# RWKV scan: backward operand rows with exchanged halves, and the Gram products of both directions side by side

## The reference, cut to what matters

```python
def rwkv7_scan(r, w, k, v, kk, a, s0):
    def step(s, inp):
        rt, wt, kt, vt, kkt, at = inp
        sa = jnp.einsum('nbhij,nbhj->nbhi', s, kkt)
        s = (s * wt[..., None, :] - sa[..., :, None] * (kkt * at)[..., None, :]
             + vt[..., :, None] * kt[..., None, :])
        return s, jnp.einsum('nbhij,nbhj->nbhi', s, rt)
```

## Time and profile before

| | us |
|---|---|
| median of 3 runs | 4274.93 (4273.5 to 4280.36) |
| the profiled execution, its own time | 4274.99 |
| its span, first to last instruction | 4273.4 |
| PE busy | 3907.9 (91%) |
| PE weight loads | 2614.5 (61%) |
| VectorE busy | 2053.0 (48%) |
| ScalarE busy | 1175.1 (27%) |
| POOL busy | 1171.8 (27%) |
| scan stage, 1285 to 2480: PE / VectorE / POOL / ScalarE busy | 1074.7 / 767.3 / 562.3 / 536.0 |

### The profile page before, as it was taken

One profiled execution on the slowest core, in us unless ns is written; L12 is line 12 of the kernel. 1 busy time (PEld: TensorE's weight loads), 2 busy tenths in 40 slices (PEclk: granted clock), 3 DMA queues, 4 the chain that ended last, 5 costly groups with the idle time before them and its releaser, 6 DMA issues. The chain is left out here.

```text
span 4273.4 us, 102696 instructions
## 1 busy us (share of the span) xinstructions
PE 3907.9 (91%) x40204; PEld 2614.5 (61%) x40204; DVE 2053.0 (48%) x3485; ACT 1175.1 (27%) x2889; POOL 1171.8 (27%) x1491
## 2 busy tenths in 40 slices
PE   7999689999997899999999959959999999999988
PEld 5888566666656898888988825435333333443333
DVE  2221277677754766667667568971111111111116
ACT  1111144454433444544444423310000000000000
POOL 0000011101110545545555434424222222222220
PEclk9999899999998999999999979978999999999999
DMA  9811366656645434434344274424668999999986
GB/s 362 202 73 53 89 221 204 210 182 202 211 159 164 132 97 131 127 121 131 105 141 134 62 204 137 136 100 150 258 256 325 403 393 401 395 407 420 420 339 244
DMA packets 318412, 908.15 MB, mean 213 GB/s; under 512 B 67288, under 2 KB 164856, under 8 KB 269296
## 3 DMA queue, kind: packets, MB, share of 16 engines
q1 hardware_dynamic: 264224, 755.00, 49.6%
q0 software_dynamic: 46928, 131.41, 8.4%
q10 hardware_dynamic: 6912, 16.78, 1.0%
HBM read 960.84 MB, written 200.17 MB: 272 GB/s over the span
## 5 line engine op out<-in xcount | busy, mean ns | idle before, releaser
L2763 PE MATMUL exp_gate_up<-exp_w_gate,exp_rows_and_rowsT 128*64 128x512 f32 x1664 | 730.9, 596 | 13.4 <-DMA exp_w_up<-in_moe_w_up_dram 12.4
L2763 PE MATMUL exp_gate_up<-exp_w_up,exp_rows_and_rowsT 128*64 128x512 f32 x1664 | 731.4, 596 | 0.0
L2763 PEld LDWEIGHTS exp_gate_up<-exp_w_gate,exp_rows_and_rowsT 128*64 128x64 f32 x1664 | 227.8, 138 | 482.9 <-issue 482.8
L2714 DVE TENSOR_TENSOR exp_hidden<-exp_hidden,exp_gate_up 64x512 f32<-64x512 f32 x104 | 71.9, 692 | 700.4 <-ACT exp_hidden L2695 700.4
L880 PE MATMUL rwp_product<-rwp_hT,rwp_w_rw 128*128 128x256 f32 x1808 | 393.9, 380 | 10.6 <-DVEq L814 10.6
L1061 PE MATMUL hgp_product<-hgp_hT,const_w_hg 128*128 128x256 f32 x1664 | 379.0, 383 | 8.7 <-DVEq L1042 8.7
L2788 PE MATMUL exp_down<-exp_w_down,exp_hiddenT 128*64 128x512 f32 x1664 | 380.0, 597 | 3.2 <-issue 0.6
L880 PEld LDWEIGHTS rwp_product<-rwp_hT,rwp_w_rw 128*128 128x128 f32 x1808 | 344.2, 191 | 57.8 <-issue 11.0
L1061 PEld LDWEIGHTS hgp_product<-hgp_hT,const_w_hg 128*128 128x128 f32 x1664 | 313.8, 192 | 60.4 <-issue 10.8
L2695 ACT ACTIVATE exp_hidden<-exp_gate_up 64x512 f32<-64x512 f32 x104 | 61.2, 589 | 944.6 <-PE exp_gate_up L2763 944.6
L2672 POOL DMA_INDIRECT s_yb<-exp_out,exp_row_slot x104 | 104.1, 1001 | 575.5 <-PE exp_rows_turned L2748 450.1
(11 more groups left out here) (426 smaller groups left out, 6920.8 us busy)
## 6 DMA issues: line engine op xcount, KB each, us to landing
exp_w_gate<-in_moe_w_gate_dram SPq DMA_DIRECT2D x208, 1024.0 KB
exp_w_up<-in_moe_w_up_dram SPq DMA_DIRECT2D x208, 1024.0 KB
exp_w_down<-in_moe_w_down_dram SPq DMA_DIRECT2D x104, 2048.0 KB
s_rw_in<-prep_operands SPq DMA_DIRECT2D x72, 514.0 KB, 3.9
rw_operands<-s_rw_in SPq DMA_DIRECT2D x72, 514.0 KB, 7.9
hg_qkf<-s_hg_in SPq DMA_DIRECT2D x36, 768.0 KB, 9.5
rw_tokens<-s_rw_tm SPq DMA_DIRECT2D x144, 192.0 KB, 4.8
prep_raw<-s_rw_lat SPq DMA_DIRECT2D x16, 1664.0 KB, 7.6
```

The lines of the kernel that those rows point to most:

```text
L2714: nc.vector.tensor_tensor(hid[u][H], hid[u][H], pgu[u][H], ALU.mult).then_inc(s["hid_ready"], 1)
L2763: i = nc.tensor.matmul(pgu[u][q:q + BLK], xT[:, k, r * BLK:(r + 1) * BLK], w[r][:, k, :], start=(k == 0), stop=(k == KD - 1))
```

## The change

A function `channels_at(d, h)` says on which half of the partitions the channels of head half h lie: for direction 0 on half h, for direction 1 on the other. `load_rows` loads each block in two transfers, one for each half, to those partitions, so that direction 1 has its halves exchanged. `gram` is called once for both directions, at the place of direction 0's call; it waits for both directions' rows and banks, and then alternates, for each pair of heads, direction 0's two matmuls and direction 1's two. Direction 1 reads the partitions of one half and writes the bank's other half, so its matmuls use the two quarters off the diagonal.

```diff
+def channels_at(d, h):
+
+    return HALF[h if d == 0 else 1 - h]
...
             for d in range(2):
                 s = self.s[d]
                 wait(sp, s["grams"], 4 * m)
-                sp.dma_start(self.row[v][d][:], self.S["rw_in"][d, bass.ds(2 * m + v, 1)].rearrange("n p x -> p (n x)")).then_inc(s[f"row_loaded{v}"], 16)
+                for h in range(2):
+                    dst = self.row[v][d][channels_at(d, h)]
+                    sp.dma_start(dst, self.S["rw_in"][d, bass.ds(2 * m + v, 1), HALF[h]].rearrange("n p x -> p (n x)")).then_inc(s[f"row_loaded{v}"], 16)
...
-        def gram(d, k, v):
-            s = self.s[d]
-            if k == 0:
-                pe.wait_ge(s[f"row_loaded{v}"], 16 * m + 16)
-            if k == 0 and v == 0:
-                wait(pe, s["r_ready"], 6 * m)
-            else:
-                pe.wait_ge(s["masked"], 4 * m + 2 * k + v)
+        def gram(k, v):
+
+            for d in range(2):
+                s = self.s[d]
+                if k == 0:
+                    pe.wait_ge(s[f"row_loaded{v}"], 32 * m + 32)
+                if k == 0 and v == 0:
+                    wait(pe, s["r_ready"], 6 * m)
+                else:
+                    pe.wait_ge(s["masked"], 4 * m + 2 * k + v)
             pe.sem_inc(self.turns, 1)
...
+            for j in range(NPAIR):
+                for d in range(2):
+                    row = self.row[v][d]
+                    left = self.part(row, "beta" if k == 0 else "kappa")
+                    both = row[:, 0:2 * XW].rearrange("p (x j t) -> p x j t", x=2, j=NPAIR)
+                    dst = self.pa[d][:].rearrange("p a b t -> p (a b t)").rearrange("p (j x t) -> p j x t", j=NPAIR, x=2)
+                    for h, q in enumerate(HALF):
+                        c = channels_at(d, h)
+                        if full:
+                            i = nc.tensor.matmul(dst[q, j].rearrange("p x t -> p (x t)"), left[c, j, :], both[c, :, j, :], start=True, stop=True)
+                        else:
+                            i = nc.tensor.matmul(dst[q, j, 0, :], left[c, j, :], both[c, 0, j, :], start=True, stop=True)
+                    if j == NPAIR - 1:
+                        i.then_inc(self.s[d]["grams"], 1)
...
                 elif name[:-2] == "gram":
-                    gram(d, int(name[-2]), v)
+                    if d == 0:
+                        gram(int(name[-2]), v)
```

More of the change, by code:

```diff
@@ L1627, in state @@
             i.then_inc(s["s_psum"], 1)
-        def gram(d, k, v):
-            s = self.s[d]
-            if k == 0:
-                pe.wait_ge(s[f"row_loaded{v}"], 16 * m + 16)
-            if k == 0 and v == 0:
-                wait(pe, s["r_ready"], 6 * m)
-            else:
-                pe.wait_ge(s["masked"], 4 * m + 2 * k + v)
-            pe.sem_inc(self.turns, 1)
-            row = self.row[v][d]
-            left = self.part(row, "beta" if k == 0 else "kappa")
-            both = row[:, 0:2 * XW].rearrange("p (x j t) -> p x j t", x=2, j=NPAIR)
-            dst = self.pa[d][:].rearrange("p a b t -> p (a b t)").rearrange("p (j x t) -> p j x t", j=NPAIR, x=2)
-            for j, q in heads:
-                if full:
-                    i = nc.tensor.matmul(dst[q, j].rearrange("p x t -> p (x t)"), left[q, j, :], both[q, :, j, :], start=True, stop=True)
-                else:
-                    i = nc.tensor.matmul(dst[q, j, 0, :], left[q, j, :], both[q, 0, j, :], start=True, stop=True)
-            i.then_inc(s["grams"], 1)
+        def gram(k, v):
[7 more added lines that the diff above has]
+                    pe.wait_ge(s["masked"], 4 * m + 2 * k + v)
+            pe.sem_inc(self.turns, 1)
+            for j in range(NPAIR):
[12 more added lines that the diff above has]
+                        i.then_inc(self.s[d]["grams"], 1)
```

## The result

The changed kernel takes 4322.92 us (median of 4 runs, 4319.18 to 4329.05) against 4275.09 us for the kernel before on the same chip: ratio 1.0112, interval 1.0097 to 1.0127. It is 47.8 us slower. The forecast was 4266.5 us with a range up to 4284, so the sign is wrong and the result lies 39 us beyond the range.

A forecast was written before the change was run, and what follows sets the result against it. ScalarE and the array were taken as equally late up to out_a, leaving only gram1b to gain: 11.2 us, less 2.6 for clock and 0.5 for row loads, 8.1 off 4274.99: 4266.5 us, range 4254 to 4284.

The forecast's parts named there:

- Row loads: Loads of row blocks in the scan: eight half-size issues, same bytes, hidden except once at the stage's start, 0.5 us.
- Speed of a step: Gram step in the scan: four quarters busy instead of two, 34 ns an instruction, 1.1 us instead of 1.77.
- rival 4: Gram step runs at 29 ns an instruction: 15 x 1.15 = 17 us gained, 4258 us; chance 0.18.
- G: Length of one new Gram step, taken as 1.1 us (0.93 to 1.24) instead of 1.77.
- quarters with shared rows take turns: Gram step stays 1.75 us, gram1b ends 1.2 us later a round: 18 us slower, 4293 us; chance 0.12.
- The joined wait: Grams wait for both directions' masks; VectorE nevertheless 0.75 us early, its mask for gram1b ending at 1864.27.
- gram1b: Last Gram step of a round: ends at 1865.47 instead of 1866.22, 0.75 us a round.
- Three of four steps are worth nothing: Shorter gram0a, gram0b and gram1a only become idle array time before out_a, which waits for ScalarE's u.
- Rival 5: The array's busy share is the bound: all 64 steps count, 43 us gained, 4232 us; chance 0.04.
- The clock: Idle gaps around out_a halve the clock every fourth round at 0.7 us: 2.6 us in all (0 to 15).
- Does it stay?: After gram1b, the rest of the round keeps the gain: 15 rounds x 0.75 = 11.2 us.

The follow-up runs named there:

- columns_split: The kernel before with each row block loaded in two transfers over all 128 partitions, half of the columns each: 4265.82 us, ratio 0.9999.
- halves_only: The kernel before with each row block loaded in two transfers of 64 contiguous partitions, nothing exchanged, Gram steps untouched: 4313.47 against 4265.83 us, ratio 1.0105.
- every_second: The kernel before with each row block loaded in two transfers of 64 partitions, the even and the odd ones: 4265.98 us, ratio 0.9998.
- join_only: The changed kernel with whole row loads and direction 1 in direction 0's two quarters, keeping joined wait and alternation: 4283.44 us, ratio 1.0034 to the kernel before.
- stored_twice: The changed kernel with the exchange made when operands are stored, direction 1's first half stored twice, whole loads: 4260.58 against 4266.21 us before; repeated, 4263.71 against 4266.33.

## Why the prediction was wrong, point by point

*The term that failed is "Row loads": "four loads become eight of half size, same bytes", hidden but for 0.5 us.* The count and the bytes were right and do cost nothing, as columns_split shows. The price lay in the partitions that each transfer fills: 210 to 250 GB/s in place of 412, or 229 in place of 359 over the whole time in which rows move, with every DMA engine busy. I priced the transfers by their bytes and asked only who waits for them. In fact nobody waits for them by name in a full round; what is hurt is the array, through the "issue" stalls in the burst (2.2 us a round more) and the half clock behind these (3.9 us a round more of it, which cost 1.4), and these leave the rest of a round 3.5 us longer. halves_only shows 47.6 us for splitting the loads alone, where the forecast had 0.5. The bound of 2.24 us for the issues was too low as well: half the rows do not issue in half the time, as eight issues took 5.08 to 6.32 us in a full round where four took 2.02 to 3.28. SyncE's queue shows the issues in the changed kernel, first those of a full round, which answer to the earlier trace rows, then the first of the stage:

```profile
1759.04 6.32 SPq L1555 DMA_DIRECT2D rw_operands<-s_rw_in  x8
...
1285.42 4.99 SPq L1555 DMA_DIRECT2D rw_operands<-s_rw_in  x8
```

At the start of the stage the four issues before took 1.77 us (at 1285.30) and the eight take 4.99. The first Gram steps and what follows come later there:

```profile
1293.24 1.13 PE L1658 MATMUL rw_inverse_bank<-rw_operands 64*64 64x64 f32 x32 [19.37 <-DMA rw_operands<-s_rw_in]
```

```profile
1300.38 1.28 ACT L449 ACT_TABLE_LOAD   x1 [25.88 <-DMA hg_v<-s_hg_v]
```

Before, these stood at 1289.03 and 1295.97. ScalarE is 4.4 us later, waiting for the other scan's loads queued behind the row loads. I had named that queue and given it 0.5 us, at most 2.24. How much of the 4.4 us is left at the first full round cannot be read from single traces, as said above.

The Trainium skill has the rule that speaks against this change (DMA: Bandwidth & Descriptors, Rules for kernel authors): of two transfers to disjoint partition halves it says "Don't bother — they serialize", and advises one of 128 partitions. halves_only agrees, 1.0105. But every_second fills disjoint halves as well, and cost nothing, so the advice holds here for contiguous halves. I had weighed a rule on the array, and not this one.

*Speed of a step: right, a little too slow.* I took 1.1 us from start to start (0.93 to 1.24). Measured are 0.92 us for gram0a and 1.04 for gram1b, 29 to 33 ns an instruction, nearer to rival 4's 29 than to my 34; that the span reads 1.10 is no support for G. The rival in which quarters with shared rows take turns is out. So is, for these steps, the rule of the Trainium skill (TensorE: Matmul & The Clock Gate, Part 3) that the prediction set beside it, that a weight load overlaps a running matmul only if their row groups differ: a weight load that waited for every matmul of its rows would have kept the step near 1.75 us.

*The joined wait and gram1b: the sum came out by luck.* The Gram segment is 0.81 us shorter in the changed kernel, 0.73 to 0.79 where loads are whole; 0.75 was forecast. But the forecast's 0.75 was a step 1.1 us long that starts 0.23 us late, behind a mask. In none of the 14 rounds of the table does gram1b wait for a mask. In 8 of them it starts as early as before (12.30 us into the segment, 12.29 before) and is 1.04 us shorter, so the segment takes 13.33 or 13.34 us against 14.37. In the other six the out step is longer, mostly by stalls without a semaphore, and takes 0.1 to 1.1 us back. The mask that did not delay it and the stalls that I had not counted cancel in the mean. VectorE in this round, in the changed kernel:

```profile
1737.97 1.29 DVE L1800 TENSOR_TENSOR rw_A_rho_beta<-rw_inverse_bank,const_before_upto 128x512 f32<-128x512 f32 x2
...
1740.64 1.29 DVE L1800 TENSOR_TENSOR rw_A_rho_beta<-rw_inverse_bank,const_before_upto 128x512 f32<-128x512 f32 x2 [0.25 <-PE rw_inverse_bank L1656]
...
1742.98 1.31 DVE L1818 COPY_PREDICATED rw_inverse<-const_level_masks,rw_A_rho_beta 128x512 f32<-128x512 uint32 x2
1744.18 0.68 DVE L582 TENSOR_TENSOR hg_exponent<-hg_logf_sum 128x512 f32<-128x512 f32 x1
...
1746.01 0.65 DVE L1800 TENSOR_TENSOR rw_kappas<-rw_inverse_bank,const_before_upto 128x512 f32<-128x512 f32 x1
```

The copies and the difference before:

```profile
1859.21 2.40 DVE L1804 COPY_PREDICATED rw_inverse<-const_level_masks,rw_A_rho_beta 128x512 f32<-128x512 uint32 x2
1861.51 1.75 DVE L582 TENSOR_TENSOR hg_exponent<-hg_logf_sum 128x512 f32<-128x512 f32 x1
```

And POOL's first scaled decays, before and in the changed kernel:

```profile
1859.60 1.42 POOL L496 TENSOR_TENSOR hg_decay_to_end<-hg_qkf,hg_decay_to_end 128x512 f32<-128x512 f32 x1 [16.29 <-ACT hg_decay_chunk L461]
1744.26 1.74 POOL L496 TENSOR_TENSOR hg_decay_to_end<-hg_qkf,hg_decay_to_end 128x512 f32<-128x512 f32 x1 [16.28 <-ACT hg_decay_chunk L461]
```

The order is as the sum assumed, but not the times: I took VectorE 0.75 us earlier and its instructions as long as before. In the kernel before, the second copy and the difference start while POOL runs and take 1.80 and 1.75 us in all 14 rounds. In the changed kernel the copy starts before POOL does and takes 0.72 in all 14, and the difference takes 0.68 in the 12 rounds in which it does, and 1.75 in the two in which it does not. The mask is ready 10.16 us into the segment in those 12 rounds, not 12.4. join_only measures the price of the joined wait where the step stays slow, 1.21 us against 1.2; there both instructions start while POOL runs and are slow, as the formula takes them.

*Three of four steps are worth nothing: right.* ScalarE's stretch kept its 10.42 us, and the gain became the wait of 1.45 us for rw_u (1.2 to 1.5 forecast). Rival 5, the busy share as the bound, is out: 35 us less busy array and no faster, and 5.6 us faster at most in stored_twice.

*The clock: wrong in place.* I feared it behind the two gaps ahead of out_a, and no kernel shows a low clock in the Gram segment, where the changed kernel has those gaps in each round. It came behind the stalls of the burst instead, and dearer: 1.4 us a round more, where the forecast had 2.6 us in all.

*Does it stay? Only partly, if at all.* With whole loads the forecast leaves 15 x 0.75 = 11.2 us less the clock. stored_twice gave 5.6 and 2.6 us, and rounds shorter by 0.49 and 0.28 us. The rest of the round gave back 0.2 to 0.6 us. Stalls while loads run fall on other steps when the array comes earlier, so I would expect some of it; but the rest scatters by as much from trace to trace, and this is argued, not shown.

*What the stalls are.* Both kernels' pages have a queue that carries instructions, in packets of 16 KB:

```profile
q8 instruction: 257, 4.21, 0.4%
```

In the full rounds of the kernel before, the array runs 254 recorded instructions (median; matmuls and weight loads) from the start of one such packet to that of the next, 64.5 bytes of packet for each, so these packets look like the array's own program. The packets' times tie the stalls to them. In the 17 traces the 14 rounds of the table have 362 "issue" gaps over 1 us, and each of the 362 ends 1.2 to 1.9 us behind the end of one of these packets. A moment taken at random in the same rounds lies there in 12 to 15% of cases, and the ends of the array's 445 other waits over 0.2 us do in 7%. The stall that ends at 1775.12 above is an example. No packet starts from 1763 to 1772; then, 2 us after the array ran dry, one does (queue, packets, MB, share, for 1772 to 1773), and the array goes on 1.44 us behind its end:

```profile
q8 instruction: 1, 0.02, 7.9%
```

The last packet before the one that ends a stall started 6.7 us earlier in the kernel before (median), 7.9 in halves_only and 8.4 in the changed kernel, so they come more slowly while the row packets are slow. The stalls keep that distance: two in one burst lie 5.5 to 6.9 us apart before and 6.5 to 9.2 in the changed kernel. That the array goes on only when such a packet has landed is shown as far as times can show it. That the packet was late because it stood behind the loads' packets in the same engines is argued: no run moved one without the other.

## What to carry to other kernels

When a load has to be split or permuted, keep each transfer spread over all partitions: split it by columns or by every second partition, or permute once when the data are stored, and never fill the halves one by one. Price a transfer by its own rate in the trace and not by its bytes alone, even if nobody waits for it, for a slow burst can starve an engine that no semaphore ties to it; look then at when the instruction packets arrive. When the array was slowed, count a stretch at half clock as half lost, and not as lost. And before counting what faster matmuls win, find the engine that releases the next one: here three of four shortened steps only moved the wait to ScalarE. And do not take an instruction's length as given when it moves: VectorE's took 0.7 or 1.8 us, by whether POOL had already begun.

## What the runs showed of the hardware that I had not expected

- Transfers that fill partitions 0 to 63 and 64 to 127 ran at 210 to 251 GB/s with all sixteen DMA engines busy, while even and odd partitions ran at 395 and halves of the columns at 358. Loads of 32 partitions kept 232, so the loss did not double.
- Stalls of the array without any semaphore reached 4.8 us in the changed kernel's burst, against 2.6 before, and the granted clock was at half behind long ones. All 362 of them over 1 us, over 17 traces, ended 1.2 to 1.9 us behind a 16 KB packet of queue q8. The idle of 1.45 us ahead of out_a in every round was followed by a clock of 1.00.
- Four quarters of the array, each row half and each column half shared by two of them, took 128 columns of fp32 at 29 to 33 ns an instruction, against 55 for two diagonal quarters.
- A predicated copy and a difference of 128x512 floats on VectorE took 1.80 and 1.75 us when they started while POOL ran its scaled decays, and 0.72 and 0.68 when they started before it.
